# First norm's modulation blocks in four places, first input block by halves of its channels, time-step products turned round

## The reference

```python
cond = jax.nn.silu(c)
mod = cond @ ada_w[layer] + ada_b[layer]          # 1024 -> 6 * 1024
shift1, scale1, gate1, shift2, scale2, gate2 = jnp.split(mod, 6, axis=-1)
h = x * (1 + scale1) + shift1                     # modulate
proj = h @ w_in                                   # z | xbc | dt_raw
xbc = jax.nn.silu(causal_depthwise_conv(xbc, conv_w, conv_b))
dt = jax.nn.softplus((dt_raw + dt_bias).astype(F32))
A = -jnp.exp(a_log.astype(F32))
dA = (dt * A)                                     # goes into the chunked scan
```

## Time and profile before

| what | value |
|---|---|
| median of 3 runs | 1934.44 us |
| profiled execution: its own time | 1936.71 us |
| profiled execution: span | 1934.9 us |
| TensorE busy | 1800.6 us (93%) |
| VectorE / ScalarE / GpSimd busy | 916.7 / 735.0 / 725.5 us |
| DMA, mean over the span | 212 GB/s |

### The profile page before, as it was taken

The page is one execution under the profiler, slowest core; times in us unless marked ns, Lnnn a source line. Parts: engine busy times, 40 slices in busy tenths (PEclk is TensorE's granted clock), DMA queues, the critical chain, the costliest instruction groups (busy, mean ns, idle before and its releaser), DMA issues. The chain is left out here.

```text
span 1934.9 us, 29376 instructions
## 1 busy us (share of the span) xinstructions
PE 1800.6 (93%) x9752; PEld 1257.9 (65%) x9752; DVE 916.7 (47%) x2029; ACT 735.0 (38%) x1889; POOL 725.5 (37%) x808
## 2 busy tenths in 40 slices
PE   1899999988999799999999999999997999999994
PEld 1644444476644388888888555558655888888882
DVE  4677764367523445344343630137544544434337
ACT  2433320065412354444544320124335444454451
POOL 4133310035312467545545150300034864555540
PEclk9799999999999899999999899999998999999997
DMA  9475646661200779999998712110108999999964
GB/s 339 149 265 207 244 166 207 212 220 44 71 11 22 289 244 351 338 334 324 325 326 244 244 51 94 46 55 1 61 33 314 289 338 320 327 331 341 343 181 163
DMA packets 169711, 409.50 MB, mean 212 GB/s; under 512 B 37620, under 2 KB 45156, under 8 KB 169620
## 3 DMA queue, kind: packets, MB, share of 16 engines
q1 hardware_dynamic: 132180, 337.77, 48.3%
q0 software_dynamic: 37440, 70.56, 14.6%
HBM read 394.23 MB, written 79.75 MB: 245 GB/s over the span
## 5 line engine op out<-in xcount | busy, mean ns | idle before, releaser
L1284 ACT ACTIVATE arena<-psum,lncol 128x128 f32<-128x128 f32 x1024 | 370.8, 467 | 416.4 <-PE psum L784 416.4
L806 PE MATMUL psum<-arena 128*128 128x128 f32 x4096 | 500.9, 278 | 0.0
L806 PEld LDWEIGHTS psum<-arena 128*128 128x128 f32 x4096 | 478.2, 192 | 1.0 <-issue 1.0
L818 PE MATMUL psum<-arena 128*128 128x512 f32 x512 | 241.1, 593 | 0.4 <-DVE arena L1823 0.4
L1805 DVE COPY arena<-arena 128x1 f32 (+1 forms) x128 | 19.7, 154 | 463.3 <-PE psum L806 332.5
L2177 POOL DMA_INDIRECT expert_sum<-arena,idx x124 | 198.9, 1604 | 40.1 <-issue 39.4
L1823 DVE SCALAR_TENSOR_TENSOR arena<-psum,arena 128x512 f32<-128x512 f32 x256 | 182.0, 743 | 14.6 <-PE psum L818 14.4
L568 PE MATMUL psum<-arena 128*128 128x512 f32 x384 | 177.4, 623 | 0.0
L784 PEld LDWEIGHTS psum<-ident,arena 128*128 128x128 f32 x1024 | 122.3, 143 | 73.4 <-issue 64.3
L2148 POOL TENSOR_TENSOR passed<-ones 128x1 f32<-128x1 f32 x252 | 50.2, 199 | 301.9 <-DVE arena L1823 290.5
L1417 DVE SCALAR_TENSOR_TENSOR arena<-arena,condT 128x512 f32<-128x512 f32 x126 | 150.7, 1196 | 11.6 <-DMA arena<-in_ada_w_dram 7.2
(11 more groups left out here) (272 smaller groups left out, 2324.4 us busy)
## 6 DMA issues: line engine op xcount, KB each, us to landing
arena<-in_moe_w_dram SPq DMA_DIRECT2D x384, 512.0 KB
arena<-in_ada_w_dram SPq DMA_DIRECT2D x32, 1024.0 KB, 5.1
arena<-in_ssm_w_in_dram SPq DMA_DIRECT2D x10, 2048.0 KB, 10.2
arena<-in_ada_w_dram SPq DMA_DIRECT2D x8, 2048.0 KB, 10.6
arena<-in_ssm_w_out_dram SPq DMA_DIRECT2D x4, 2048.0 KB, 9.6
expert_sum<-arena SPq DMA_DIRECT2D x4, 2048.0 KB, 15.4
arena<-expert_sum SPq DMA_DIRECT2D x16, 512.0 KB, 5.7
arena<-in_kv_ada_w_dram SPq DMA_DIRECT2D x4, 1024.0 KB, 5.5
```

Of the source, the lines that this page charges most:

```text
L806: mm = pe.matmul(psum[:, b, 0:P], w[:, k, :], xeT[u % 2][:, k, :], start=(k == 0), stop=(k == KC - 1))
L818: mm = pe.matmul(psum[:, b, :], aT[u % 2], exp_w[u][:, 2, 512 * n:512 * n + 512], start=True, stop=True)
L1284: ins = act.activation(xeT[u % 2][:, k, :], psum[:, b, P * j:P * j + P], ACT.Identity, scale=h_scale(l, k), bias=h_shift(l, k))
```

## The change

- `FIRST` = (0, 2, 1, 3): the first four modulation blocks are all summed by VectorE (`first_sum`), into four buffers of their own, and used in four places: `first_block(0)` before x is turned, `first_block(1)` behind the first half of the transposes, `first_block(2)` and `first_block(3)` between products of the first item. ScalarE and GpSimd have none of them.
- x is loaded as two halves of its channels instead of four token tiles, and turned by channel block (`turn_x(k)`: four transposes into one bank); it is moved 128x512 at a time (`move_modulated`).
- The first input item is computed by halves of its input channels: 16 products of k = 0 to 3 into banks 0 to 3, which stay open, and later the 16 of k = 4 to 7 into the same banks. It is loaded in two 1 MB halves.
- The time-step products are turned round: `wdt` (32 columns) is the stationary operand and HT's 512 columns the moving one, 8 products behind the first item; the 32x512 result is copied to `dtT` by ScalarE and turned back by four small transposes (`turn_dt`) behind the third half item. Softplus and dA (`steps_of_time`) run behind the seventh convolution instead of before the first.
- Pairs of modulation blocks: seven instead of eight, behind half items 2, 3, 5, 6, 8, 9, 11. Blocks alone: ten instead of eight, behind z tiles 1, 3, 4, 6, 7, 9, 11, 12, 14, 15 (counted over the 16 tiles of the z items), so that four times two neighbouring tiles have one each.
- The small vectors and `wdt` are loaded behind the first item instead of before it.

```diff
...
+        ada_first = [ada_dve, ada_pool[0], ada_pool[1], view(32, KC, 512)]
...
-        ADA_FIRST = 4
-        ADA_PAIRED = 20
-        def ada_beside(n, half):
-            h = 2 * n + half
-            return () if h % 3 == 2 else (ADA_FIRST + 2 * (h - h // 3), ADA_FIRST + 2 * (h - h // 3) + 1)
-        def ada_beside_z(n, half):
-            return ADA_PAIRED + 2 * n + half
+        FIRST = (0, 2, 1, 3)
+        ADA_FIRST = len(FIRST)
+        ADA_PAIRED = 18
+        PAIR_AT = (2, 3, 5, 6, 8, 9, 11)
+        ALONE_AT = (1, 3, 4, 6, 7, 9, 11, 12, 14, 15)
+        def ada_beside(h):
+            if h not in PAIR_AT:
+                return ()
+            a = ADA_FIRST + 2 * PAIR_AT.index(h)
+            return (a, a + 1)
+        def ada_beside_z(n, t):
+            return tuple(ADA_PAIRED + i for i, at in enumerate(ALONE_AT) if at == T * n + t)
         def ada_engine(a):
         def ada_count(a):
-            return a // 2 if a < ADA_PAIRED else a - ADA_PAIRED // 2
-        ADA_OF = (len(ada_blocks) - ADA_PAIRED // 2, ADA_PAIRED // 2)
+            return (a - ADA_FIRST) // 2 if a < ADA_PAIRED else a - ADA_PAIRED + len(PAIR_AT)
+        ADA_OF = (len(PAIR_AT) + len(ALONE_AT), len(PAIR_AT))
...
-            for a in range(ADA_FIRST):
-                ada(a)
-            def x_loaded(t):
-                if t == 0:
-                    pe.wait_ge(x_in, 16 * T)
-            turn("hT0", X, x_loaded)
-            for t in range(T):
-                turned("hT0", t)
+            def first_block(i):
+                pe.wait_ge(first_summed, i + 1)
+                ps = claim(7)
+                for j in range(4):
+                    mm = pe.matmul(ps[:, j:j + 1], ada_acc[i % 2][:, P * j:P * j + P], ones[:, 0:1], start=True, stop=True)
+                fill(mm, 7, ("mod",) + ada_blocks[FIRST[i]])
+            def turn_x(k):
+                ps = claim(k)
+                for t in range(T):
+                    mm = pe.transpose(ps[:, TILES[t]], X[:, t, P * k:P * k + P], ident[:, :])
+                fill(mm, k, ("hT0", k))
+            first_block(0)
+            pe.wait_ge(x_in[0], 16)
+            for k in range(KC // 2):
+                turn_x(k)
+            first_block(1)
+            pe.wait_ge(half_in, 16)
+            for j in range(4):
+                ps = claim(j)
+                for k in range(KC // 2):
+                    if j == 0:
+                        until_drained(pe, ("hT0", k))
+                    if (j, k) == (3, 2):
+                        first_block(3)
+                    pe.matmul(ps[:, :], ring[0][:, k, P * j:P * j + P], HT[:, k, :], start=(k == 0), stop=False)
+                if j == 1:
+                    first_block(2)
+                    pe.wait_ge(x_in[1], 16)
+                    for k in range(KC // 2, KC - 1):
+                        turn_x(k)
+            turn_x(KC - 1)
+            kind = items[0][0]
+            w, tag = take(kind)
+            for j in range(4):
+                for k in range(KC // 2, KC):
+                    if j == 0:
+                        until_drained(pe, ("hT0", k))
+                    mm = pe.matmul(psum[:, j, :], w[:, k, P * j:P * j + P], HT[:, k, :], start=False, stop=(k == KC - 1))
+                fill(mm, j, ("xbc", 4 * kind[1] + j))
+            done_item(tag, ("xbc", 4 * kind[1] + 3))
             pe.wait_ge(small_in, SMALL)
             ps = claim(6)
-            for t in range(T):
-                for k in range(KC):
-                    mm = pe.matmul(ps[:, HEADS * t:HEADS * (t + 1)], HT[:, k, P * t:P * t + P], wdt[:, k, :],
-                                   start=(k == 0), stop=(k == KC - 1))
-            fill(mm, 6, "dt")
-            at = 0
-            nb = 0
+            for k in range(KC):
+                mm = pe.matmul(ps[0:HEADS, :], wdt[:, k, :], HT[:, k, :], start=(k == 0), stop=(k == KC - 1))
+            fill(mm, 6, "dtT")
+            def turn_dt():
+                until_drained(pe, "dtT")
+                ps = claim(7)
+                for t in range(T):
+                    mm = pe.transpose(ps[:, HEADS * t:HEADS * t + HEADS], dtT[0:HEADS, TILES[t]], ident[0:HEADS, 0:HEADS])
+                fill(mm, 7, "dt")
+            at = 1
+            nb = 4
...
-                            for a in ada_beside(at, j // 2):
+                            for a in ada_beside(2 * at + j // 2):
                                 ada(a)
+                            if (at, j) == (1, 1):
+                                turn_dt()
...
-                        if t % 2:
-                            ada(ada_beside_z(kind[1], t // 2))
+                        for a in ada_beside_z(kind[1], t):
+                            ada(a)
...
+            def move_modulated(k, scale, shift):
+                ps = until_filled(act, ("hT0", k))
+                act.activation(HT[:, k, :], ps, ACT.Identity, scale=mod[:, scale + k:scale + k + 1],
+                               bias=mod[:, shift + k:shift + k + 1]).then_inc(drained[MARK[("hT0", k)][0]], 1)
...
-            for a in range(1, ADA_FIRST, 2):
-                ada_scale(a)
-            for v in (SHIFT1, SCALE1):
-                until_mod(0, v)
-            move_modulated("hT0", 0, HT, MODC[(0, SCALE1)], MODC[(0, SHIFT1)])
-            act.wait_ge(small_in, SMALL)
-            act.activation(negA[:, :], alog_bc, ACT.Exp).then_inc(soft_act, 1)
-            soft[0] += 1
-            softplus_act(dtx[:, :, :].rearrange("p a b -> p (a b)"), P, lambda: until_drained(act, "dt"))
-            softplus_ln(P, 1)
...
+            for half in range(2):
+                until_first(half)
+                for k in range(4 * half, 4 * half + 4, 2):
+                    move_modulated(k, MODC[(0, SCALE1)], MODC[(0, SHIFT1)])
...
+                        if n == 4:
+                            ps = until_filled(act, "dtT")
+                            act.activation(dtT[0:HEADS, :], ps[0:HEADS, :], ACT.Copy).then_inc(drained[MARK["dtT"][0]], 1)
+                        if n == 7:
+                            steps_of_time()
...
+            def first_sum(i):
+                acc, w = ada_acc[i % 2], ada_first[i]
+                dve.wait_ge(first_in[i][0], 16)
+                step(dve.tensor_scalar(acc, w[:, 0, :], condT[:, 0:1], None, ALU.mult))
+                for k in range(1, KC):
+                    if k == KC // 2:
+                        if i % 2:
+                            ada(*ada_blocks[FIRST[i - 1]])
+                        dve.wait_ge(first_in[i][1], 16)
+                    settle()
+                    ins = dve.scalar_tensor_tensor(acc, w[:, k, :], condT[:, k:k + 1], acc, ALU.mult, ALU.add)
+                    if k < KC - 1:
+                        step(ins)
+                ins.then_inc(first_summed, 1)
...
-            for a in range(0, ADA_FIRST, 2):
-                ada_sum(a)
-                for i in (a, a + 1):
-                    ada(*ada_blocks[i])
-            until_mod(0, SHIFT1)
-            until_mod(0, SCALE1)
-            move_modulated("hT0", 1, HT, MODC[(0, SCALE1)], MODC[(0, SHIFT1)])
...
+            for half in range(2):
+                first_sum(2 * half)
+                first_sum(2 * half + 1)
+                ada(*ada_blocks[FIRST[2 * half + 1]])
+                until_first(half)
+                for k in range(4 * half + 1, 4 * half + 4, 2):
+                    move_modulated(k, MODC[(0, SCALE1)], MODC[(0, SHIFT1)])
...
+                        if n == 7:
+                            steps_of_time()
...
-            for a in range(1, ADA_PAIRED, 2):
-                pool.wait_ge(ada_scaled, a // 2 + 1)
-                w = ada_pool[a // 2 % 2]
+            for a in range(ADA_FIRST + 1, ADA_PAIRED, 2):
+                done = ada_count(a)
+                pool.wait_ge(ada_scaled, done + 1)
+                w = ada_pool[done % 2]
                 for n in (4, 2):
                     step(pool.tensor_tensor(w[:, 0:n, :], w[:, 0:n, :], w[:, n:2 * n, :], ALU.add))
                     settle()
-                if a >= 2:
-                    until_filled(pool, ("mod",) + ada_blocks[a - 2])
+                until_filled(pool, ("mod",) + ada_blocks[a - 2 if done else FIRST[-1]])
...
+            def load_first(i):
+                for half, rows_ in enumerate(HALVES):
+                    sp_.dma_start(ada_first[i][:, rows_, :], ada_cols(FIRST[i])[:, rows_, :]).then_inc(first_in[i][half], 16)
+            def load_x(half):
+                R = slice(512 * half, 512 * half + 512)
+                sp_.dma_start(X[:, :, R], x[0].rearrange("(t p) d -> p t d", p=P)[:, :, R]).then_inc(x_in[half], 16)
+            def load_item_0(half, done):
+                sp_.dma_start(ring[0][:, HALVES[half], :], items[0][1][:, HALVES[half], :]).then_inc(done, 16)
+            load_first(0)
+            load_first(1)
+            load_x(0)
+            load_item_0(0, half_in)
+            load_first(2)
+            load_x(1)
+            load_first(3)
```

(61 more changed lines are left out.)

64 lines of the change are left out of this document (30 added, 34 removed).

## The result

| | before | changed | ratio, 95% interval |
|---|---|---|---|
| first set of runs | 1935.02 us | 1901.38 us (1897.33 to 1903.68) | 0.9822 [0.9804, 0.9841] |
| once more, beside the experiments | 1935.54 us | 1895.44 us (1893.05 to 1903.51) | 0.981 [0.9783, 0.9836] |

The change makes the kernel 34 to 40 us faster. 1896 was forecast, with a range of 1886 to 1909.

The account below looks back on a forecast made before the run. The start was held bound by load order, later xbc items partly by waits for VectorE's sums and half clock. Stage times summed to a scan start of 353.8 instead of 392.03, 38.2 us less: median 1896, range 1886 to 1909.

Parts of the forecast that it names:

- The start: Loading through time steps: MBs land every 2.69 us, first 512-column product at 26.4, item 1 at 66.8 us.
- Clock in the start: TensorE's first work at half clock: 16 transposes at 0.20 us each, then 3 products in 5.1 us.
- Rival A: Clock falls in stretches of short work between long products: 5 us each, 1901 or 1906; chance 25%.
- the two mixed stretches: Block 2 with 12 transposes, and the pair of half item 2 with `turn_dt`: about 2.2 us short work each.
- VectorE's sum about 84.5 to 94.5: Sum for the pair before half item 4, partly beside GpSimd, said to be in time for 98.7 us.
- The pattern of the pairs: From half item 4 on: half items without, with, with a pair, 50.3 us a period, waits and half clock included.
- z items: Stage before the scan: 117.3 us plus two blocks and half clock, 121.1 in all, ending at 353.8.
- rival B: Neighbouring z blocks come late: four places wait and lose the clock, 20 us, so 1916; chance 6%.
- C: The 2.44 us waits shrink too: three waits, pair and clock, 15 us at most; chance 5%.
- D: Clock not released in item 0: 1928, or 1955 with all of item 1 slow as well; chance 4%.
- E: Start fails: x's first half does not land fifth, first product near 40 us, 14 us lost, 1910; chance 2%.
- The rest: Scan behind the z items: the change has no instruction there, so it was only shifted as it is.

Follow-up runs that it names:

- first profile: Profiled execution of the changed kernel from its first set of runs, nothing further changed: 1903.38 us.
- second profile: Profiled execution of the same changed kernel, run again beside the experiments, nothing further changed: 1895.44 us.
- added products: Changed kernel plus 11 unread 512-column products in TensorE's idle start, 8 before block 0 and 3 behind it: 1895.69 us.
- earlier sums: Changed kernel with VectorE's sum and ScalarE's scaling for pairs of half items 5, 8, 11 one tile earlier in their lists: 1886.03 us.

## Why the prediction was right

*The start* was right to 0.7 us at item 1 in the first profile and 2.7 too late in the second (64.06 against 66.8), so the close hit is in part luck. The experiments show what its terms are worth: the order of the loads 9.4 us at item 1, the halves of item 0 11.2 (3.4 more for each against the second profile), the turned time steps about 3. They are not parts of one sum, as each one needs the others' cover. The other parts of the change (all four first blocks summed by VectorE, the new places of the later blocks, the small vectors behind the first item) were not tried by themselves.

*Clock in the start.* Half clock at a printed 1.00 was right, as the added products show. Its length was taken from one row; it varies between executions by nearly 3 us at this place (10.02 and 7.10 for the same eight products).

*Rival A* was half right: the clock fell, but not in the two mixed stretches, in either profile. It fell in the first profile behind the pair of half item 3, after 0.34 us of waiting and 1.81 of short work, and cost 1.7 us, not 5. The fall that the rival meant does exist: with the added products it came behind the pair of half item 2 with `turn_dt` (15.70 for 14.00 us, in the version with them alone and in one of the two profiles with the earlier sums). It too cost 1.7.

*The step that was mis-sized*: "VectorE's sum about 84.5 to 94.5, a part of it beside GpSimd". It ended at 97.7. I had spread 12.45 us evenly over seven steps, but the price falls on three steps, each as long as the GpSimd instruction that it meets, so a partial overlap costs as much as a full one. That made the wait of 0.34 us. The same wait stands in the second profile (0.35), where the clock did not fall; so it costs 0.3 us in both and 1.7 more in one.

*The pattern of the pairs* stayed: 2.45, 2.43 and 2.45 us of waiting, before half items 5, 8 and 11. Two stretches of the same shape took 52.4 (99.58 to 152.00) and 50.8 us (to 202.80) against the mean of 50.3 that was used; the first with the fall of the clock in it.

*z items*: 121.55 us against 121.1. No wait for a sum between neighbouring tiles: rival B did not come. Rivals C, D and E did not either; C's waits went only with an edit of the lists. Two statements on the range were wrong: 1886 was called half of C's 15 us and is two thirds of them (half is 1888.5), and E, at 1910, lies outside the range of 1886 to 1909 like B and D.

*The rest*: 1.4 us more in the first profile and 1.6 less in the second (1893.6 - 352.3 = 1541.3) than before. Which of the later falls of the clock make that was not followed up.

## What to carry to other kernels

When a start is bound by loads, put the MBs in the order in which a first piece of real work can be made of them, and cut that work (here by input channels, with the sums left open in PSUM) so that it needs half of everything. Judge a cut by what is queued behind it too: the time-step edit gave 5.7 us at its place in the old kernel and 2 to 3 in the end, because VectorE's sum was late next. And where one engine starts a long sum behind a step that waits for TensorE, try moving it one step up in its list: here three waits of 2.45 us went by that alone, with the sum as long as before.

## What was not expected of the hardware

- A VectorE step with both inputs in the buffer, 0.77 us alone, took 4.88, 2.72 and 1.64 us when it met GpSimd instructions of 4.85, 2.67 and 1.59 us.
- Short products kept the clock at 1.00 for some 6 us before it fell (64 records of 32 columns), and a pair of 1.84 us without a wait never lost it in the changed kernel's two profiles; yet a pair with 0.34 us of waiting lost it in one execution and not in another of the same program.
- The printed clock of the first 26 us is 1.00 while the same 16 transposes take 3.67 us cold and 1.97 us behind added products.
